# Padding two row-turning steps of a two-layer hybrid encoder from 40 to 128 columns and turning them by transposes

## The reference, cut to what matters

```python
x = x + 0.5 * swiglu(rmsnorm(x), ...)            # FFN, D_FF = 2816
proj = rmsnorm(x) @ w_in                         # z, xbc, dt, q, f, i, g
y = [ssd_mixer(z, xbc, dt), hgrn2_mixer(q, f, i, g)]
x = x + y @ w_out
x = x + 0.5 * swiglu(rmsnorm(x), ...)            # FFN
```

## Time and profile before

| | |
|---|---|
| median of 3 runs | 1944.68 us (1942.98 to 1945.22) |
| the profiled execution: time | 1943.6 us |
| its span, first to last instruction | 1941.9 us |
| TensorE matmuls | 1932.7 us busy, 10408 records |
| VectorE | 756.5 us busy |
| ScalarE | 695.5 us busy |
| GpSimd | 905.8 us busy |
| DMA | 181.75 MB moved |

### The profile page before, as it was taken

One profiled execution on the slowest core, in us unless ns is written; L12 is line 12 of the kernel. 1 busy time (PEld: TensorE's weight loads), 2 busy tenths in 40 slices (PEclk: granted clock), 3 DMA queues, 4 the chain that ended last, 5 costly groups with the idle time before them and its releaser, 6 DMA issues.

```text
span 1941.9 us, 28643 instructions
## 1 busy us (share of the span) xinstructions
PE 1932.7 (100%) x10408; PEld 1585.2 (82%) x10408; DVE 756.5 (39%) x1228; ACT 695.5 (36%) x965; POOL 905.8 (47%) x550
## 2 busy tenths in 40 slices
PE   9999999999999999999999999999999999999999
PEld 7888888888788888888888888888877888888887
DVE  6222221389875322231132222114888752222312
ACT  5222222364533322222332222224555433223223
POOL 3444444466335544444444444545653444444444
PEclk9999999999999999999999999999999999999999
DMA  5222333222113332333322233332221123222332
GB/s 187 98 98 97 93 99 97 90 77 80 64 55 98 108 97 97 96 90 99 107 88 98 97 97 92 91 102 88 73 89 56 65 89 117 97 97 89 95 99 97
DMA packets 53499, 181.75 MB, mean 94 GB/s; under 512 B 6816, under 2 KB 6816, under 8 KB 53408
## 3 DMA queue, kind: packets, MB, share of 16 engines
q1 hardware_dynamic: 53264, 180.56, 28.9%
q10 hardware_dynamic: 144, 0.00, 0.0%
HBM read 178.45 MB, written 2.10 MB: 93 GB/s over the span
## 4 chain that ended last, share of the span: by engine, by line
PE 92%; DVE 4%; issue 2%; ACT 1%; DMA 0%; DVEq 0%; SPq 0%; ACTq 0%
PE ps L1456 29%; PE ps L1458 29%; PE ps L1457 29%; PE ps L1578 1%; PE ps L1580 1%; PE ps L1579 1%; DVE w L1139 1%; PE ps L1773 0%; PE ps L1934 0%; DVE g L1002 0%; PE ps L1778 0%; PE ps L1757 0%; DVE e L1110 0%; DVE bf L1063 0%; DVE g L1008 0%
## 5 line engine op out<-in xcount | busy, mean ns | idle before, releaser
L481 POOL TENSOR_TENSOR wlo<-raw,whi 128x1024 fp32r<-128x1024 f32 (+1 forms) x536 | 903.5, 1702 | 1028.0 <-ACT whi L542 554.4
L1456 PE MATMUL ps<-hhi,whi 128*128 128x512 f32 x1760 | 692.0, 393 | 2.5 <-DVE wlo L877 1.6
L1458 PE MATMUL ps<-hhi,wlo 128*128 128x512 f32 x1760 | 685.4, 389 | 0.0
L1457 PE MATMUL ps<-hlo,whi 128*128 128x512 f32 x1760 | 685.1, 389 | 0.0
L1456 PEld LDWEIGHTS ps<-hhi,whi 128*128 128x128 f32 x1760 | 330.4, 188 | 80.8 <-issue 10.4
L1458 PEld LDWEIGHTS ps<-hhi,wlo 128*128 128x128 f32 x1760 | 330.4, 188 | 70.0
L1457 PEld LDWEIGHTS ps<-hlo,whi 128*128 128x128 f32 x1760 | 330.6, 188 | 66.5
L536 ACT ACTIVATE whi<-raw 128x1024 fp32r<-128x1024 f32 x168 | 177.2, 1055 | 280.2 <-PE ps L1458 258.2
L1456 PE MATMUL ps<-ahi,whi 128*128 128x512 f32 x704 | 273.9, 389 | 0.0
L1457 PE MATMUL ps<-alo,whi 128*128 128x512 f32 x704 | 273.9, 389 | 0.0
L1458 PE MATMUL ps<-ahi,wlo 128*128 128x512 f32 x704 | 273.9, 389 | 0.0
(11 more groups left out here) (264 smaller groups left out, 1365.1 us busy)
## 6 DMA issues: line engine op xcount, KB each, us to landing
raw<-in_up SPq DMA_DIRECT2D x168, 512.0 KB, 3.2
raw<-in_mix SPq DMA_DIRECT2D x64, 512.0 KB, 3.3
raw<-in_dn SPq DMA_DIRECT2D x64, 448.0 KB, 3.3
raw<-in_dn SPq DMA_DIRECT2D x32, 512.0 KB, 3.5
raw<-in_lead SPq DMA_DIRECT2D x8, 512.0 KB, 3.2
x<-in_x SPq DMA_DIRECT2D x8, 256.0 KB, 5.9
raw<-in_lead SPq DMA_DIRECT2D x8, 256.0 KB, 6.0
raw<-in_mix SPq DMA_DIRECT2D x8, 256.0 KB, 2.5
```

The costliest lines, as they stand in the source:

```text
L481: low = pool.tensor_tensor(wlo[:, q, part], raw[:, q, part], whi[:, q, part].bitcast(F32), ALU.subtract)
L1456: mm(dst, whi[:, q, s], mh, start=start, stop=False)
L1457: mm(dst, whi[:, q, s], ml, start=False, stop=False)
L1458: return mm(dst, wlo[:, q, s], mh, start=False, stop=stop)
```

## The change

The tiles `pick2`, `acbs`, `hrow`, `rhl`, `hpick` and `ahl` get 128 where they had 40, rows or columns. `ahl` is now 2 KB a partition and moves to a free place in the arena. The two turning steps use `pe.transpose` (one record each) in place of float32 matmuls against the identity, and write 128 partitions of the bank.

```diff
-        pick2 = sb("pick2", [40, 8], F32R)
+        pick2 = sb("pick2", [P, 8], F32R)
-        acbs = sb("acbs", [40, T], F32R)
+        acbs = sb("acbs", [P, T], F32R)
-        ahl = place("ahl", [P, TC, 40], 11, F32R)
+        ahl = place("ahl", [P, TC, P], 16, F32R)
-        hrow = put("hrow", [40, T], 46, F32R)
-        rhl = put("rhl", [P, TC, 40], 48, F32R)
-        hpick = put("hpick", [40, 2 * NP, HALF], 50, F32R)
+        hrow = put("hrow", [P, T], 46, F32R)
+        rhl = put("rhl", [P, TC, P], 48, F32R)
+        hpick = put("hpick", [P, 2 * NP, HALF], 50, F32R)
...
-                        do(acb_split, acbs[:], bank(3)[0:40, :], ACT.Copy)
+                        do(acb_split, acbs[:], bank(3), ACT.Copy)
...
-                            do(head_rows, hrow[:], bank(6)[0:40, :], ACT.Copy)
+                            do(head_rows, hrow[:], bank(6), ACT.Copy)
...
-            did(tt(pick2[:], ident[0:40, 0:8], ident[0:40, 32:40], ALU.add))
+            did(tt(pick2[:], ident[:, 0:8], ident[:, 32:40], ALU.add))
...
-                    did(dve.tensor_copy(hpick[:], pick2[:].bitcast(F32).unsqueeze(2).to_broadcast([40, 2 * NP, HALF])))
+                    did(dve.tensor_copy(hpick[:], pick2[:].bitcast(F32).unsqueeze(2).to_broadcast([P, 2 * NP, HALF])))
...
-                        last = mm(bank(3)[0:40, cols_of(c)], ahl[:, c, :].bitcast(F32), ident[:], start=True, stop=True)
+                        last = pe.transpose(bank(3)[:, cols_of(c)], ahl[:, c, :].bitcast(F32), ident[:])
...
-                        mm(bank(4 + h), pick2[:, k:k + 1].to_broadcast([40, P]), acbs[:],
+                        mm(bank(4 + h), pick2[:, k:k + 1].to_broadcast([P, P]), acbs[:],
...
-                        last = mm(bank(6)[0:40, cols_of(c)], rhl[:, c, :].bitcast(F32), ident[:], start=True, stop=True)
+                        last = pe.transpose(bank(6)[:, cols_of(c)], rhl[:, c, :].bitcast(F32), ident[:])
```

## The result

| | before | after |
|---|---|---|
| median | 1944.65 us (1942.98 to 1946.32, 12 runs) | 1948.70 us (1947.36 to 1950.41, 12 runs) |
| ratio after to before | | 1.0022, 95% interval 1.0014 to 1.0031 |
| span of the profiled execution | 1941.9 us | 1946.9 us |

A forecast was written before the change was run, and what follows sets the result against it. TensorE was taken as the bound: its stream shortens 6.4 us, but VectorE limits the gain to 1.88 + 0.28 = 2.16 us a layer, 4.3 us for two, giving 1940.4 us from 1944.68; range 1937.6 to 1943.8 us.

The forecast's parts named there:

- The turns: `sums_turn` and `head_turn`: four transposes replace eight matmul records, each saving 0.75 us of TensorE's stream, 1.50 us a layer.
- The spreads: Matmuls reading `pick2` and `hpick`: 128 rows avoid a change of array shape; 3 x 0.38 and 2 x 0.20 + 0.14 us.
- the zero for p = 0: `ssd_turn` spreads at p = 0: no gain, since `head_sums` comes next and starts when ScalarE's copy ends.
- The rival that only the turns count: 40 rows cause no change of shape, so the spreads gain nothing: 3.0 us saved, 1941.7 us; chance 0.24.
- VectorE's additions: Two clears grow from 160 to 512 elements, 0.29 us more each; `hpick` on 128 partitions adds nothing, at most 0.25 us.
- The cover: VectorE's 1.70 us wait for the transposes of `ssd_turn(1)` hides the second clear, with 0.66 us of it left.
- What is late next: `ssd_outs(3)` needs VectorE's `ssd_y` 1: of 1.30 us saved after the ties, TensorE keeps 0.28 and waits 1.0 us.
- The tie at `ssd_turn(1)`: VectorE waits 1.70 us for TensorE at 509.54 us, so savings before it carry over to VectorE.
- that at the evacuation of xs2: VectorE's 0.49 us wait for TensorE at 515.81 us; 0.1 us was to be left, so the tie holds.
- the 1.0 forecast: A new TensorE wait of about 1 us in each layer for VectorE's line 1262, in front of `ssd_outs(3)`.
- the first paragraph: What bounds the kernel: TensorE busy practically the whole span at full clock, one 0.3 us wait in the first layer's mixer.
- The rival for slower, the clock: New transposes drop the clock from 2.4 to 1.2 GHz behind each turn; one block at each of four, 1962 us; chance 0.04.

The follow-up runs named there:

- e1: Changed kernel with sixteen redundant waits (8 filler TensorE instructions) at the start of `sums_turn`; 1941.21 us, ratio 0.9984.
- e6: e1 with the clear of `rhl` and the copy into `hpick` moved in front of `ready(seg_exp)` of `ssd_main(0)`; 1939.89 us, ratio 0.9980.
- e5: e1 with `ssd_norm(0)` and `ssd_norm(1)` moved right behind `ssd_states(3)`; 1938.71 us, ratio 0.9977.
- e4: Kernel before without four low-by-high matmuls of the first value block, 8 TensorE instructions less a layer; 1951.04 us, ratio 1.0030.
- e2: Changed kernel with `rhl`, `hrow`, `hpick` and `head_turn` as in the kernel before; 1949.36 us, ratio 1.0025.

## Why the prediction was wrong

**The turns, 1.50 us a layer: right for `sums_turn`**, to 0.01 us. `head_turn` got shorter by as much, but gave 0.3 us back in a wait for `st`.

**The spreads, 1.14 + 0.54 us: right**, each to 0.01 us, the zero for p = 0 included; `head_sums` still starts when ScalarE's copy ends. The rival that only the turns count is out: a spread of 40 rows does cost its change of shape on both sides.

**VectorE's additions: mis-sized.** The clear was right at 0.29 us. What hung on it was missed: the two small instructions behind it slid into GpSimd's time, 1.03 us more. The cover held all the same: of VectorE's wait for the transposes of `ssd_turn(1)` 1.1 us are left in e1. What it cost was `head_turn`, which comes earlier and needs `st`, and which I hadn't set against VectorE's delay: 0.3 us a layer, and e6 takes that wait away.

**What is late next: right in place.** The tie at `ssd_turn(1)` holds, that at the evacuation of xs2, of which 0.1 us was to be left, is gone from VectorE's waits. TensorE waits for line 1262, 0.73 us by the profile (0.8 by the start) for the 1.0 forecast. e5, which moves those two instructions, removes that wait, but half of it comes back behind it, so VectorE's work as a whole sets the limit there and not the order of these two alone.

**Sum without the fetch.** 2 x 2.16 us were forecast; the mixer stages of e1, which has the change's parts and the old place of the block's end, are 2 x 2.0 us shorter, its median 3.4 us (by the ratio 3.1). The stream's 3.18 us less the 0.32 at `head_turn`, the 0.8 at line 1262 and 0.23 that came in front of the transposes of `ssd_turn(3)` make 1.8 us; the rest is mostly a shorter pause in the scores (by 0.16 and 0.06 us). That the sum comes so close to 2.16 is in part luck: two waits that weren't forecast against one that was forecast 0.2 us too long, and the pause.

**The step that failed** is the first paragraph: "a microsecond taken out of TensorE's stream is a microsecond of the result, as long as no other engine is so close behind". TensorE's own instruction supply was left out. The change was costed by the durations of the records that went, never by their number. The kernel before showed the warning: a wait of L1661 for "issue" of up to 0.4 us, in the very list from which only the wait of L1786 was read. In its place stand, against the kernel before, a pause longer by 2.2 and 1.9 us, and a granted clock of half for 3.4 us in each layer, which costs 1.55 and 1.50 us. Together 7.2 us; the rest of the two stages is 3.8 us shorter, and -3.8 + 7.2 = +3.4 us is what the mixer stages are longer (1.8 and 1.6 us). The medians differ by 4.05 us, with an interval of 2.7 to 6.0.

**The rival for slower, the clock:** its effect came, its cause didn't. It put the lapse behind the transposes; it came behind the pause, without transposes too (e4), and not at all with transposes and no long pause (e1).

**Open.** Why eight instructions move the transfer's start by 2.5 us isn't shown: the trace has no row for where the sequencer stands. Whether another count would remove the last 0.2 us wasn't tried, nor was a move of `head_sums` to save its wait of 0.5 us.

## What to carry to other kernels

On an engine with nothing to spare, count the instructions that a change removes or adds ahead of dense groups of tiny matmuls, not only their time: a pause inside such a group whose place moves by the number of instructions removed is the mark of instruction fetch. A few filler instructions ahead are a cheap test and, as here, a mend, but any later edit to the engine's program can undo it. When a wait is removed by moving work on another engine, look for it further on, in the weight loads too: here half came back. And where shapes change between neighbours, measure from start to start: without the fetch the change saves 1.9 us a layer, where the eight matmul records that went take 0.88.

## What the runs showed of the hardware that I had not expected

- TensorE can run dry of instructions for up to 3.0 us in a group that takes 176 matmul records in 1.95 us when nothing stops it, and goes on 1.2 to 1.5 us after the end of the 16 KB transfer.
- Pauses of up to 1.1 us left the clock at 2.4 GHz; with pauses of 2.4 to 3.0 us came 1.2 GHz for 3.4 or 6.8 us, in both layers of all four kernels that had them. In six of the eight the clock fell 0.9 to 1.7 us after TensorE went on and stayed down for 3.4 us; in the first layer of e2 and the second of e4 it fell 0.3 and 0.7 us before and stayed down for 6.8 us. In the changed kernel 3.4 us of it cost 1.5 us.
- A step from 128 rows to 40 costs 0.17 us on entry behind the transposes. On leaving, behind a 512-column matmul, the first product starts 0.09 us later and the second 0.10 us later still. The spreads' own records are as long as before (0.50 us for one).
- Two VectorE instructions on 128 x 32 elements took 0.73 and 0.68 us beside GpSimd, and 0.18 and 0.19 us apart from it.
